# A decoder trunk in Strassen-Winograd products: C11 built on a PSUM copy, another order of loads and branch sums, and two merging additions by accumulating transfers

## The chip, the cores and the metric

The kernel runs on one core of one Trainium2 chip. The metric is device time in microseconds (us), the median of three runs: 780.66 us before the change (779.02 to 780.73). The engines are PE (TensorE, matrix multiply), ACT (ScalarE), DVE (VectorE), POOL (GpSimd) and SP (SyncE, which issues transfers). SP and POOL each have a queue of transfers of their own; the same 16 DMA engines serve both.

## The reference, cut to what matters

```python
# D_MODEL 1024, SEQ 512, DEPTH 1, 16 heads of 64, window 128, D_FF 4096, all float32
h = rmsnorm(x, attn_norm_g)
u_b, u_c, u_x, q, k, v, g_conv, g_attn = split(h @ w_in)
y_conv = (u_b * short_conv(u_c * u_x, conv_w)) @ w_conv_out
attn   = sliding_window_attention(q, k, v, attn_sinks, rel_bias)
y_attn = attn @ w_attn_out
mixed  = sigmoid(g_conv) * y_conv + sigmoid(g_attn) * y_attn
x = x + mixed @ w_o
h2 = rmsnorm(x, mlp_norm_g)
x = x + square(relu(h2 @ w_up)) @ w_down
return rmsnorm(x, final_norm_g)
```

The merge of the two branches, `mixed`, and the five products around it (`g_conv`, `g_attn`, `y_conv`, `y_attn`, `mixed @ w_o`) are the part that the change touches.

## The kernel before, in words

**The first 232 us.** x is normed and transposed; w_in's columns for k, v, q and the convolution go through `transposed_strip`, with the attention of four blocks of 128 queries woven in (`mixer_block`). In the last block `transpose_probs(3, qd)` and `values(3, qd)` for the quads qd = 2 and 3 are left over and are issued among the products that follow. POOL's `mask(n, qd)` zeroes the part of the transposed probabilities outside the window; it is an affine select of the high part, then one of the low part, and `values` waits for both.

**The stages.** From then on the work is 13 stages, each a product of a 512 x 1024 by a 1024 x 1024 matrix: GC and GA (the two gates), CO and AO (the outputs of the two branches), WO (the output projection), then four pairs of w_up and w_down slices. Each stage is one level of Strassen-Winograd: seven products named M1, N2, M6, M5, M7, M3, N4, in this order on PE. The moving operands are B11, B21, T2, T1, T3, B22 and T4, where B11 to B22 are the four blocks of the weights (1 MB each) and T1 to T4 are sums of them. The stationary operands are corners of the activations or sums of them (S1 to S4). For GC and GA, which share their activations, these sums are made once, written to memory, and brought back by SP (`load_sum`, 1 MB for each of M6, M5, M7 and M3) when the attention's tiles under them are free: that of M7 after `values(3, 3)`.

**Two parts of each operand.** A float32 number is split in a high and a low part. ACT makes the high part (`high_part` for weights, L1133; `s_high` for activations, L1210), DVE subtracts it for the low part (`low_part`, L1679; `s_low`, L1734). A product is three kinds: high by high, activation low by weight high, activation high by weight low. Each kind is eight matrix multiplies of 128 x 512, four for each half b of the tokens. The tile `high` has two buffers, so the high part of product n waits until product n-2 has ended.

**The sums of the weights.** T2 = B11 + T3 (`sum_t2`, L1656) and T4 (`sum_t4`, L1673) are DVE additions. T1 and T3 are made by transfers that POOL issues: T3 as one accumulating transfer onto B12 (L612), T1 as a plain transfer (L631) and, when that has landed, an accumulating one onto it (L635). In stage GC the second transfer of T1 stands behind the last `mask` in POOL's program.

**The results.** A stage's four corners are C11 = M1 + N2, C12, C21 (the end of the chain N4) and C22. M1, M6, M7 and N4 accumulate on one pair of PSUM banks, the chain; N2 has a pair of its own, M5 and M3 the third. ACT copies M1 to zc11, M1 + M6 (negated) to zc12 and M5 to zc22 (`copy_out`, L1223), and DVE adds the rest: `sum_c11` (L1824), `sum_c22` (L1830), `sum_c12` (L1835). PE waits for `sum_c22` before it issues N4, since that sum reads the chain.

**The merge.** In GC and GA the corners go through a sigmoid (`gate`). `gate_conv` (L1851) multiplies the corners of CO by the first gate, `gate_attn` (L1858) those of AO by the second, and `merge` (L1865) adds the two on DVE, in the order of corners C11, C22, C12, C21 (numbers 0 to 3). PE transposes each merged corner (`mixed_transposes`, L826): corner 0 behind M5 of AO, corner 1 inside N4 of AO, corners 2 and 3 inside M1 of WO.

**What sets the order.** Every engine's program is written out by hand, and each instruction waits on semaphores. Nothing is reordered at run time: an instruction that waits holds all behind it on its engine. After WO the stages repeat one pattern.

Of the kernel before, what the change touches and what calls it, by code (L numbers as in the profile page):

```python
# [12 lines left out]
P = 128  # L13
# [108 lines left out]

def slot_of(s, i):

    return part_no(s, i) % 3
# [54 lines left out]
def build(nc, x, attn_norm_g, w_in, conv_w, w_conv_out, attn_sinks, rel_bias, w_attn_out, w_o,  # L180
          mlp_norm_g, w_up, w_down, final_norm_g, out):
    ctx = ExitStack()
    with ctx:
# [44 lines left out]
        slot_at = [two_at + 2 * KT * T * i for i in range(3)]  # L228
# [15 lines left out]
        b2_sum, b1_sum = (place(n, [P, 4, 2 * P], offset=two_at + 6 * KT * T + o) for n, o in  # L244
                          (("b2_sum", 0), ("b1_sum", KT * T)))
# [88 lines left out]
        mix_t, mix_ready = sem("mix_t"), sem("mix_ready")  # L334
# [10 lines left out]
        copied, summed, relu_done = sem("copied"), sem("summed"), sem("relu_done")  # L345
# [63 lines left out]
        def sum_of(s, which):  # L409

            return {2: b2_sum, 1: b1_sum}[which] if s < WO else {2: m2_sum, 1: m1_sum}[which]
# [11 lines left out]
        def attn_gate(at_):  # L423

            part, (i, j) = at_ % 2, ((1, 0), (0, 0))[at_ // 2]
            return four_of(gates[:, part, :, :], i, j)
# [28 lines left out]
        def _(sp):  # L455
# [114 lines left out]
        def _(pool):  # L570
# [45 lines left out]
            for n in range(1, TB):  # L616
                if n == 2:
                    add_t3(GC)
                for qd in range(QUADS if n < TB - 1 else QUADS - 1):
                    mask(n, qd)  # L620

            for s in range(STAGES):
# [28 lines left out]
        def _(pe):  # L651
# [219 lines left out]
            def product(s, i, fresh, between={}):  # L871
# [4 lines left out]
                else:  # L876
# [46 lines left out]
            for s in range(STAGES):  # L923
                if is_up(s):
# [17 lines left out]
                    pe.wait_ge(summed, 3 * g + 2)  # L942
                    up_product(s, N4, False)
                    continue
                if s < WO:
                    if s == GA:
                        pe.wait_ge(pv_out, QUADS * TB)
                    elif s == CO:
                        pe.wait_ge(summed, 1)
                    elif s == AO:  # L950
                        pe.wait_ge(summed, 3 * GA + 1)
                    product(s, M1, True)
                    if s == GC:
# [21 lines left out]
                    pe.wait_ge(copied, 3 * s + 3)  # L975
                    product(s, M3, False)
                    pe.wait_ge(summed, 3 * s + 2)
# [4 lines left out]
                pe.wait_ge(summed, 3 * up_no(s - 1) + 1)  # L982
# [12 lines left out]
                pe.wait_ge(summed, 3 * up_no(s - 1) + 3)  # L995
# [13 lines left out]
        def _(act):  # L1009
# [125 lines left out]
            def mixer_block(n, it, before):  # L1135
# [26 lines left out]
                probs_hi(n, 1)  # L1162
                lo_share(n, 1)
# [7 lines left out]
            def gate(s, at_):  # L1171

                i, j = CORNERS[at_]
                if at_ < 3:
                    act.wait_ge(summed, 3 * s + at_ + 1)
# [15 lines left out]
            def s_high(s, i):  # L1191
# [14 lines left out]
                if at_ < 3:  # L1206
                    wait_used(act, GA, {M1: M5, N2: M7, M6: M3}[i])
# [928 lines left out]
```

## Time and profile before

| what | value |
|---|---|
| three runs, median (lowest, highest) | 780.66 us (779.02, 780.73) |
| the profiled execution's own time | 779.52 us |
| its span, first to last instruction | 777.7 us |
| mean granted TensorE clock | 0.991 |
| PE busy | 751.2 us, 97% |
| DVE busy | 650.7 us, 84% |
| ACT busy | 418.4 us, 54% |
| POOL busy | 82.9 us, 11% |
| PE idle before stationary loads of the products, put down to "issue" | 11.9 us |

A row of the timeline gives the start in us, the duration, the engine, the line of the kernel, the operation with output and input, and, in square brackets, how long the engine sat idle before it and what ended that. A matmul row's duration overlaps the next by a part, since matmuls are pipelined: the distance of two starts tells more than the duration. One kind of a product goes by in 1.81 us, a product in 5.44 us, at full clock.

### The profile page before, as it was taken

Reading aid. Unit: us, or ns where it says so; the run is one execution under the profiler, and the core shown is the slowest. Engines: PE = TensorE matmul, PEld = TensorE weight load, DVE = VectorE, ACT = ScalarE, POOL = GpSimd, SP = SyncE. Lnnn points to the kernel's source line nnn. Section 1 sums busy time; section 2 is a strip of 40 time slices with the busy share of each in tenths; the row PEclk is TensorE's granted clock in tenths of the full one; section 3 lists DMA queues with packets and bytes.
Section 4 is the critical chain, followed back from the end, with each engine's and each line's share of the span. In section 5 each row is a group of like instructions: output and inputs, shape, how many; then the busy total and the mean of one; then the engine's idle time right before and its main releaser. Section 6 shows DMA issues by size and latency. Waiting matters only on the chain.

```text
span 777.7 us, 10470 instructions
## 1 busy us (share of the span) xinstructions
PE 751.2 (97%) x4067; PEld 649.5 (84%) x4067; DVE 650.7 (84%) x752; ACT 418.4 (54%) x530; POOL 82.9 (11%) x117
## 2 busy tenths in 40 slices
PE   8999999999999499999997999999999999999996
PEld 7888888888887388887785899988998899889985
DVE  5766788988897365989999899998699969995997
ACT  7424555544534355665564778554555455535456
POOL 3202000111014010101010100101010101010102
PEclk9999999999999799999999999999999999999999
DMA  7737413161238776767592766677767767777702
GB/s 258 231 99 267 149 55 108 55 163 54 81 112 300 183 208 163 217 173 212 187 279 76 176 184 182 169 208 177 204 165 195 184 181 198 188 191 193 207 7 109
DMA packets 69408, 131.22 MB, mean 169 GB/s; under 512 B 2604, under 2 KB 22132, under 8 KB 69364
## 3 DMA queue, kind: packets, MB, share of 16 engines
q1 hardware_dynamic: 50400, 84.18, 32.7%
q0 software_dynamic: 18752, 46.15, 26.9%
q8 instruction: 30, 0.49, 0.2%
q10 hardware_dynamic: 212, 0.28, 0.1%
q14 instruction: 14, 0.11, 0.1%
HBM read 124.29 MB, written 6.32 MB: 168 GB/s over the span
## 4 chain that ended last, share of the span: by engine, by line
PE 83%; DVE 9%; issue 3%; DMA 2%; ACT 1%; POOL 0%; SPq 0%; DVEq 0%; ACTq 0%
PE pair L898 35%; PE pair L863 21%; PE pair L672 7%; PE pair L674 7%; PE pair L673 7%; DVE home_lo L1679 2%; DMA home_raw<-in_w_attn_out 2%; PE pair L719 1%; DVE s_lo_tile L1734 1%; PE pair L694 1%; DVE home_raw L1673 1%; PE pair L693 1%; PE pair L703 1%; DMA xn<-in_x 1%; DVE home_raw L1656 1%
## 5 line engine op out<-in xcount | busy, mean ns | idle before, releaser
L1133 ACT ACTIVATE high<-home_raw 128x2048 fp32r<-128x2048 f32 x91 | 174.3, 1915 | 172.6 <-PE pair L898 114.8
L1679 DVE TENSOR_TENSOR home_lo<-home_raw,high 128x2048 fp32r<-128x2048 f32 x91 | 208.5, 2291 | 47.1 <-ACT high L1133 46.7
L898 PE MATMUL pair<-high,s_hi_tile 128*128 128x512 f32 x440 | 111.9, 396 | 11.9 <-issue 9.8
L898 PE MATMUL pair<-high,s_lo_tile 128*128 128x512 f32 x440 | 111.3, 394 | 2.9 <-DVE s_lo_tile L1734 2.9
L898 PE MATMUL pair<-home_lo,s_hi_tile 128*128 128x512 f32 x440 | 110.3, 392 | 0.5 <-DVE home_lo L1679 0.5
L898 PEld LDWEIGHTS pair<-high,s_hi_tile 128*128 128x128 f32 x440 | 82.8, 190 | 30.4 <-issue 11.9
L672 PE MATMUL pair<-h,wgt 128*128 128x512 f32 x256 | 101.5, 397 | 0.0
L898 PEld LDWEIGHTS pair<-high,s_lo_tile 128*128 128x128 f32 x440 | 83.3, 190 | 21.2 <-DVE s_lo_tile L1734 3.8
L674 PE MATMUL pair<-h,wgt 128*128 128x512 f32 x256 | 99.9, 390 | 0.0
L673 PE MATMUL pair<-h,wgt 128*128 128x512 f32 x256 | 99.8, 390 | 0.0
L898 PEld LDWEIGHTS pair<-home_lo,s_hi_tile 128*128 128x128 f32 x440 | 83.1, 189 | 18.3 <-DVE home_lo L1679 0.9
L863 PE MATMUL pair<-h_hi,home_lo 128*128 128x256 f32 x448 | 58.4, 283 | 0.0
L863 PE MATMUL pair<-h_lo,high 128*128 128x256 f32 x448 | 58.4, 283 | 0.0
L863 PE MATMUL pair<-h_hi,high 128*128 128x256 f32 x448 | 58.3, 283 | 0.0
L674 PEld LDWEIGHTS pair<-h,wgt 128*128 128x128 f32 x256 | 48.1, 188 | 10.5
L863 PEld LDWEIGHTS pair<-h_hi,high 128*128 128x128 f32 x448 | 56.0, 192 | 0.3
L673 PEld LDWEIGHTS pair<-h,wgt 128*128 128x128 f32 x256 | 48.2, 188 | 9.2
L863 PEld LDWEIGHTS pair<-h_hi,home_lo 128*128 128x128 f32 x448 | 55.8, 192 | 0.0
L863 PEld LDWEIGHTS pair<-h_lo,high 128*128 128x128 f32 x448 | 55.8, 192 | 0.0
L672 PEld LDWEIGHTS pair<-h,wgt 128*128 128x128 f32 x256 | 48.1, 188 | 9.1
L1465 DVE TENSOR_TENSOR wgt<-raw,wgt 128x1024 fp32r<-128x1024 f32 x33 | 39.0, 1221 | 8.6 <-ACT wgt L1027 8.4
L1027 ACT ACTIVATE wgt<-raw 128x1024 fp32r<-128x1024 f32 x33 | 33.2, 1056 | 21.2 <-PE pair L674 21.1
(211 smaller groups left out, 1007.9 us busy)
## 6 DMA issues: line engine op xcount, KB each, us to landing
raw<-in_w_in SPq DMA_DIRECT2D x34, 512.0 KB, 4.6
home_raw<-in_w_up SPq DMA_DIRECT2D x16, 1024.0 KB, 5.5
home_raw<-in_w_down SPq DMA_DIRECT2D x16, 1024.0 KB, 5.4
home_raw<-in_w_up POOLq DMA_DIRECT2D x12, 1024.0 KB, 8.1
home_raw<-in_w_down POOLq DMA_DIRECT2D x12, 1024.0 KB, 8.5
home_raw<-in_w_in POOLq DMA_DIRECT2D x7, 1024.0 KB, 8.8
home_raw<-in_w_in SPq DMA_DIRECT2D x7, 1024.0 KB, 5.1
home_raw<-in_w_conv_out SPq DMA_DIRECT2D x4, 1024.0 KB, 5.1
```

The source lines that it names most:

```text
L672: mm(bank[j][:, :], wh, rhs[:, 0, k, :], start=(k == 0), stop=False)
L673: mm(bank[j][:, :], wh, rhs[:, 1, k, :], start=False, stop=False)
L674: last = mm(bank[j][:, :], wl, rhs[:, 0, k, :], start=False, stop=(k == KT - 1))
L693: mm(acc, q, khi[:, kg, keys], start=True, stop=False)
L694: last = mm(acc, q, klo[:, kg, keys], start=False, stop=True)
L703: last = nc.tensor.transpose(bank[B_PT][:, c * P:(c + 1) * P], pr[:, qd % 2, i, P:2 * P], ident[:, :])
L863: last = mm(acc[:, f, :], w[:, k, f * P:(f + 1) * P], a_[:, k, :], start=(fresh and kind == 0 and k == 0 and f % 2 == 0), stop=(kind == 2 ...
L898: last = mm(pair[region(s, i)][:, b, :], a_[:, k, b * P:(b + 1) * P], w[:, k, :], start=(fresh and kind == 0 and k == 0), stop=(kind == 2 ...
L1027: a(wgt[weight_slot(s1)][:, 0, 1024 * e:1024 * e + 1024], raw[raw_slot(c1)][:, :], ACT.Copy).then_inc(hi_ready, 1)
L1133: a(high[n % 2][:, :], home_raw[home_of(s, name)][:, :], ACT.Copy).then_inc(m_hi, 1)
L1465: v.tensor_tensor(w[:, 1, 1024 * e:1024 * e + 1024], raw[raw_slot(2 * s1 + e)][:, :], f32(w[:, 0, 1024 * e:1024 * e + 1024]), ALU.subtract ...
L1679: v.tensor_tensor(home_lo[home][:, :], home_raw[home][:, :], f32(high[n % 2][:, :]), ALU.subtract).then_inc(m_lo, 1)
```

## The change: what it does

1. **C11 on a copy in PSUM** (stages GA, CO, AO). ACT's `seed` copies M1's two halves from the chain to N2's pair, half b when M1's half b has ended. N2 then accumulates on the copy (`fresh` is false), with its kinds in the order high and activation-low of half 0, the same of half 1, then weight-low of both. Its first matmul of half 0 waits for `half_copied`, that of half 1 for `copied`. `copy_out` of M1 and `sum_c11` are gone from these stages; `gate`, `gate_conv` and `gate_attn` read corner 0 in PSUM.
2. **GC's first products.** N2 follows M1 directly; `values(3, 2)` and `transpose_probs(3, 3)` stand behind N2 and `values(3, 3)` behind M6. ACT makes N2's high part earlier, DVE puts `sum_t4` and `low_part(N2)` ahead of `probs_lo(3, 2)`.
3. **Loads.** In GC, POOL issues T1's first transfer ahead of `mask(3, 2)` and its accumulating one ahead of `mask(3, 3)`. SP loads GA's B12 ahead of B11.
4. **Branch sums.** S2 and S1 of CO and AO move to free corners of `gates`, the activation parts get five slots instead of three in these stages (`PART_SLOTS`), and `s_high`, `s_low`, s1 to s4, `gate` and the sums of results stand elsewhere in ACT's and DVE's programs.
5. **Two merges by transfer.** Corners 0 and 1 are added by an accumulating transfer from `gates` to `mixed` (0.5 MB each) that POOL issues: merge(0) behind T1 of AO, merge(1) between the two transfers of T1 of WO. Corners 2 and 3 stay on DVE.

```diff
-    return part_no(s, i) % 3
+    n = part_no(s, i)
+    return PART_SLOTS[n] if n < len(PART_SLOTS) else n % 3
...
+            sp.wait_ge(t_ready, 4 * (TB - 1) + 3)
+            load_sum(HS.index(M5))
+            load_block(GA, 0, 1)
             wait_strip(sp, S_OUT - 1)
             sp.wait_ge(m_lo, 1)
             load_block(GA, 0, 0)
-            sp.wait_ge(t_ready, 4 * (TB - 1) + 3)
-            load_sum(HS.index(M5))
-            load_block(GA, 0, 1)
...
+            def merge(at_):
+
+                pool.wait_ge(weighed, at_ + 1)
+                pool.wait_ge(gated, at_ + 1)
+                pool.dma_start(four_of(mixed, *CORNERS[at_]), attn_gate(at_), accum_op=ALU.add).then_inc(mix_added, 16)
...
                 if s == GC:
-                    mask(TB - 1, QUADS - 1)
+                    mask(TB - 1, 2)
+                if s == WO:
+                    merge(1)
                 pool.wait_ge(t1_base, 16 * (s + 1))
                 pool.dma_start(home_rows(home_of(s, "T1")), weights(s, 0, 1), accum_op=ALU.add).then_inc(t1_in, 16)
+                if s == AO:
+                    merge(0)
+                if s == GC:
+                    mask(TB - 1, 3)
...
-                pe.wait_ge(mix_done, at_ + 1)
+                pe.wait_ge(mix_added, 16 * (at_ + 1)) if at_ < 2 else pe.wait_ge(mix_done, at_ - 1)
...
+                if seeded(s) and i == N2:
+                    order = [(0, 0), (0, 1), (1, 0), (1, 1), (0, 2), (1, 2)]
...
+                    if seeded(s) and i == N2 and kind == 0:
+                        pe.wait_ge(copied, copied_no(s, 1)) if b else pe.wait_ge(half_copied, s)
...
+            def seed(s):
+
+                if s == AO:
+                    act.wait_ge(gated, 4)
                 else:
+                    act.wait_ge(gate_done, 4 * s)
+                for b in range(2):
+                    act.wait_ge(prod, 14 * s + 2 * M1 + b + 1)
+                    a(pair[region(s, N2)][:, b, :], pair[region(s, M1)][:, b, :], ACT.Copy
+                      ).then_inc((half_copied, copied)[b], 1)
```

POOL's program at the head of the stages, before and then after: `pt` is the tile of probabilities that `mask` works on, home_raw_97 and then home_raw_99 the place of T1.

```order
L607 AFFINE_SELECT pt<-pt 128x512 [waits pt_hi]
L607 AFFINE_SELECT pt<-pt 128x512 [waits pt_ready]
L631 DMA home_raw_97<-in_w_in 128x4x512 [waits half_ready1]
L607 AFFINE_SELECT pt<-pt 128x512 [waits pt_hi]
L607 AFFINE_SELECT pt<-pt 128x512 [waits pt_ready]
L635 DMA home_raw_97<-in_w_in 128x4x512 [waits t1_base]
```

```order
L668 DMA home_raw_99<-in_w_in 128x4x512 [waits half_ready1]
L638 AFFINE_SELECT pt<-pt 128x512 [waits pt_hi]
L638 AFFINE_SELECT pt<-pt 128x512 [waits pt_ready]
L674 DMA home_raw_99<-in_w_in 128x4x512 [waits t1_base]
L638 AFFINE_SELECT pt<-pt 128x512 [waits pt_hi]
L638 AFFINE_SELECT pt<-pt 128x512 [waits pt_ready]
```

Each of T1's two transfers stands one `mask` further ahead than it did.

DVE's program in stage GA, from the sum T2 of the next stage (L1656, then L1710) to the sum C22 (the row that writes zc22): L1679 and L1733 are `low_part`, L1734 and L1788 `s_low` of CO. First before, then after.

```order
L1656 TENSOR_TENSOR home_raw_94<-home_raw_92,home_raw_97 128x2048
L1755 SCALAR_TENSOR_TENSOR b_sum<-y 128x1024
L1679 TENSOR_TENSOR home_lo_107<-home_raw_93,high_120 128x2048
L1734 TENSOR_TENSOR s_lo_tile_76<-y,s_hi_tile_73 128x1024
L1830 TENSOR_TENSOR zc_85<-zc_85,pair 128x1024
L1679 TENSOR_TENSOR home_lo_112<-home_raw_98,high_121 128x2048
```

```order
L1710 TENSOR_TENSOR home_raw_96<-home_raw_94,home_raw_99 128x2048
L1733 TENSOR_TENSOR home_lo_109<-home_raw_95,high_122 128x2048
L1788 TENSOR_TENSOR s_lo_tile_82<-y,s_hi_tile_77 128x1024
L1823 TENSOR_TENSOR y<-y,gates 128x4x256
L1788 TENSOR_TENSOR s_lo_tile_78<-gates,s_hi_tile_73 128x1024
L1733 TENSOR_TENSOR home_lo_114<-home_raw_100,high_123 128x2048
L1884 TENSOR_TENSOR zc_89<-zc_89,pair 128x1024
```

Between the T2 sum and the C22 sum stood two small instructions and one `low_part`; now three small ones and two `low_part` stand there, the second that of N4, which came behind the C22 sum.

## Rows read from the trace of the kernel before

**Rows 1.** The page: the chain that ended last, by engine.
```profile
PE 83%; DVE 9%; issue 3%; DMA 2%; ACT 1%; POOL 0%; SPq 0%; DVEq 0%; ACTq 0%
```
**Rows 2.** Timeline of PE, stages GC to WO; idle time in brackets.
```profile
232.63 2.10 PE L898 MATMUL pair<-high,h 128*128 128x512 f32 x8
...
263.81 3.75 PE L898 MATMUL pair<-high,s_hi_tile 128*128 128x512 f32 x8 [9.76 <-issue]
...
287.81 3.79 PE L898 MATMUL pair<-high,h 128*128 128x512 f32 x16
...
298.69 1.98 PE L898 MATMUL pair<-high,g_hi 128*128 128x512 f32 x8
...
325.90 1.98 PE L898 MATMUL pair<-high,s_hi_tile 128*128 128x512 f32 x8
...
359.48 2.11 PE L898 MATMUL pair<-high,s_hi_tile 128*128 128x512 f32 x8 [0.77 <-DVE zc L1830]
...
365.05 1.98 PE L898 MATMUL pair<-high,s_hi_tile 128*128 128x512 f32 x8
...
421.12 3.09 PE L898 MATMUL pair<-high,s_lo_tile 128*128 128x512 f32 x8 [2.46 <-DVE s_lo_tile L1734]
...
438.27 1.98 PE L898 MATMUL pair<-high,s_hi_tile 128*128 128x512 f32 x8
```
**Rows 3.** Timeline of ACT, stages GC and GA.
```profile
239.93 0.60 ACT L1112 ACTIVATE pt<-pair 128x512 fp32r<-128x512 f32 x1
...
261.80 1.91 ACT L1133 ACTIVATE high<-home_raw 128x2048 fp32r<-128x2048 f32 x1 [12.56 <-DMA home_raw<-in_w_in]
...
298.95 1.92 ACT L1133 ACTIVATE high<-home_raw 128x2048 fp32r<-128x2048 f32 x1 [2.61 <-PE pair L898]
```
**Rows 4.** Timeline of POOL, stage GC.
```profile
237.93 0.78 POOL L631 DMA_DIRECT2D home_raw<-in_w_in  x1
240.61 0.88 POOL L607 TENSOR_SCALAR_AFFINE_SELECT pt<-pt 128x512 fp32r<-128x512 f32 x1 [1.90 <-ACT pt L1112]
245.19 2.62 POOL L607 TENSOR_SCALAR_AFFINE_SELECT pt<-pt 128x512 fp32r<-128x512 f32 x1 [3.70 <-DVE pt L1613]
247.76 1.30 POOL L635 DMA_DIRECT2D home_raw<-in_w_in  x1
```
**Rows 5.** Line L635 in 230 to 270 us: issue to landing, one transfer.
```profile
DMA to landing us min/median/max: 14.0/14.0/14.0
```
**Rows 6.** Line L612: issue to landing at 304.1 and at 382.9 us.
```profile
DMA to landing us min/median/max: 8.1/8.1/8.1
DMA to landing us min/median/max: 16.8/16.8/16.8
```
**Rows 7.** Line L635 at 283.2 and at 358 to 361 us: issue to landing.
```profile
DMA to landing us min/median/max: 10.2/10.2/10.2
DMA to landing us min/median/max: 11.6/11.6/11.6
```
**Rows 8.** Stretches: us, busy of each engine, PEclk, DMA share, GB/s.
```profile
258.00:262.00 4.00, 0.00 (x0) 0.00 (x0) 0.00 (x0) 0.20 (x1) 0.00 (x0) 0.52 1.09 288
...
397.00:401.00 4.00, 4.00 (x19) 3.30 (x19) 3.97 (x4) 0.98 (x1) 0.00 (x0) 1.00 0.99 352
...
421.00:425.00 4.00, 3.88 (x11) 3.10 (x12) 4.00 (x5) 2.32 (x3) 0.00 (x0) 0.62 0.00 0
```
**Rows 9.** Timeline of DVE, end of the attention and stage GA.
```profile
234.67 0.84 DVE L1622 TENSOR_TENSOR qa<-pair,pv_low 64x256 f32<-64x256 f32 x2
...
312.35 2.29 DVE L1656 TENSOR_TENSOR home_raw<-home_raw,home_raw 128x2048 f32<-128x2048 f32 x1 [2.87 <-DMA home_raw<-in_w_conv_out]
314.56 1.22 DVE L1755 SCALAR_TENSOR_TENSOR b_sum<-y 128x1024 f32<-128x1024 f32 x1
315.70 2.29 DVE L1679 TENSOR_TENSOR home_lo<-home_raw,high 128x2048 fp32r<-128x2048 f32 x1
...
319.04 1.22 DVE L1830 TENSOR_TENSOR zc<-zc,pair 128x1024 f32<-128x1024 f32 x1
```

More of the change, by code:

```diff
@@ L120, in drained_before, with part_before, seeded, summed_no @@
     return 0 if s == WO else 8 + 6 * ((s - WO) // 2 - 1)
+PART_SLOTS = (3, 4, 0, 1, 2, 3, 4) + (0, 1, 2, 4, 0, 1, 2) + (4, 0, 1, 2, 0, 1, 2)
 def slot_of(s, i):
-    return part_no(s, i) % 3
+    n = part_no(s, i)
+    return PART_SLOTS[n] if n < len(PART_SLOTS) else n % 3
+def part_before(s, i):
+    n, slots = part_no(s, i), [slot_of(p, k) for p in PARTED for k in range(7)]
+    before = [m for m in range(n) if slots[m] == slots[n]]
+    if not before:
+        return GA, {3: M6, 4: M5, 0: M5, 1: M7, 2: M3}[slots[n]]
+    return PARTED[before[-1] // 7], before[-1] % 7
+def seeded(s):
+    return GA <= s <= AO
+def summed_no(s, k):
+    if s > AO:
+        return 9 + 3 * (up_no(s) - 4) + k
+    return 3 * s - max(s - 1, 0) + k - (1 if seeded(s) else 0)
+def copied_no(s, k):
+    return 3 * up_no(s) + k
 def home_of(s, name):
@@ L409, in sum_of @@
         def sum_of(s, which):
-            return {2: b2_sum, 1: b1_sum}[which] if s < WO else {2: m2_sum, 1: m1_sum}[which]
+            if s < WO:
+                return four_of(gates[:, 2 - which, :, :], 1, 0 if s == CO else 1)
+            return {2: m2_sum, 1: m1_sum}[which]
         def part_source(s, i):
@@ L1173, in gate @@
                 i, j = CORNERS[at_]
-                if at_ < 3:
-                    act.wait_ge(summed, 3 * s + at_ + 1)
+                if at_ == 0 and s == GA:
+                    wait_used(act, s, N2)
+                    src = four(region(s, N2))
+                elif at_ < 3:
+                    act.wait_ge(summed, summed_no(s, at_ + 1))
                     src = (zc11, zc22, zc12)[at_]
@@ L1288, in _ @@
             s_high(AO, M3)
+            s_high(AO, N4)
             high_part(AO, M3)
@@ L1877, in relu @@
                                        op1=ALU.mult).then_inc(relu_done, 1)
+            sum_t4(GC)
+            low_part(GC, N2)
             probs_lo(3, 2)
             normalise(3, 3)
-            sum_t4(GC)
-            low_part(GC, N2)
+            low_part(GC, M6)
+            probs_lo(3, 3)
             attention_out(3, 2)
-            probs_lo(3, 3)
-            low_part(GC, M6)
-            attention_out(3, 3)
             sum_c11(GC)
             low_part(GC, M5)
+            attention_out(3, 3)
             low_part(GC, M7)
@@ L1894, in _ @@
             low_part(GA, M1)
+            s3(CO)
+            sum_c12(GC)
             sum_t4(GA)
-            sum_c12(GC)
             low_part(GA, N2)
-            s3(CO)
+            s2(CO)
+            s1(CO)
             low_part(GA, M6)
-            sum_c11(GA)
+            s3(AO)
             low_part(GA, M5)
             low_part(GA, M7)
+            s_low(CO, M1)
             sum_t2(CO)
-            s2(CO)
             low_part(GA, M3)
-            s_low(CO, M1)
+            s_low(CO, N2)
+            s4(CO)
+            s_low(CO, M6)
+            low_part(GA, N4)
             sum_c22(GA)
-            low_part(GA, N4)
-            s_low(CO, N2)
-            s1(CO)
+            s_low(CO, M5)
             low_part(CO, M1)
+            s_low(CO, M7)
             sum_c12(GA)
@@ L1934, in _ @@
             gate_conv(1)
-            s_low(AO, M1)
+            s_low(AO, M6)
+            low_part(AO, M1)
             sum_c12(CO)
-            low_part(AO, M1)
             gate_conv(2)
-            s_low(AO, N2)
             gate_conv(3)
@@ L1942, in _ @@
             low_part(AO, N2)
-            s_low(AO, M6)
-            s1(AO)
             low_part(AO, M6)
-            s4(AO)
             s_low(AO, M5)
-            sum_c11(AO)
+            gate_attn(0)
             low_part(AO, M5)
-            gate_attn(0)
-            merge(0)
             s_low(AO, M7)
```

138 lines of the change are left out of this document (64 added, 74 removed).

## The prediction, made before the changed kernel ran

> **What bounds the kernel now.** I read the chain of waits first: PE holds 83% of it, DVE 9%, "issue" 3% [rows 1]. So only idle time of PE, slow stretches of its clock, and what DVE makes it wait for can be won; work taken from ACT, DVE or POOL counts only where PE waits for it. The timeline of PE then shows where it stands still in the stages that the change touches [rows 2]. The reader is to see one large hole, 9.76 us ahead of M5 of stage GC at 263.81, and small ones around the merge, the largest 2.46 us at 421.12. Between 263.81 and 415 PE loses hardly a us: seven products of stage GA take 325.90 - 287.81 = 38.09 us, so 5.44 us each and 1.81 us a kind. Third, the engines behind the holes. The hole in GC says "issue", but ACT's high part of M5 starts at 261.80, after 12.56 us of waiting for a transfer of w_in, which is T1 [rows 3]. T1's accumulating transfer was issued at 247.76, behind `mask(3, 3)`, whose last select began at 245.19 [rows 4], and took 14.0 us to land [rows 5]. Last, the clock: 0.52 in the second half of that hole, and 0.62 at 421 to 425, after holes of the merge [rows 8]. M5's first kind took 3.75 us [rows 2].
>
> All sums are against the profiled execution, 779.52 us for a span of 777.7; the median of the three runs, 780.66, lies 1.1 us above it.
>
> **Stage GC: minus 12.0 us.** With the new order POOL issues T1's first transfer when the last strip has ended, at 231.4 (M1 of GC starts at 232.63, behind 1.3 us of values and transposes [rows 2]) instead of 237.93 [rows 4]. The accumulating one then waits for `mask(3, 2)`, which waits for `probs_lo(3, 2)` on DVE, now behind `sum_t4` and `low_part(N2)`: two big DVE instructions, 2.2 us each back to back (312.35 to 314.56; a small one takes 1.13, 314.56 to 315.70 [rows 9]), from the end of the row at 234.67, 235.5, give 240.0, the low half 0.6, the select 0.9, so 241.4 for the issue instead of 247.76. Landing: 8.1 us for 1 MB accumulated alone [rows 6], 10.2 and 11.6 with another load beside it [rows 7], 14.0 in the old place, where four sums, a block and T3 went with it [rows 5]. Now block B22 goes beside it and the sums only later: I take 10.6, landing at 252.0, plus ACT's 1.9 [rows 3]: M5 can start at 254.0. PE gets there as follows: M1 from 232.6, N2, quad 2's values and transposes (1.3), M6, quad 3's values (0.9): 232.6 + 3 x 5.44 + 2.2 + 0.1 = 251.3. So a wait of 2.7 is left, then four products: GA's M1 starts at 254.0 + 21.8 = 275.8 instead of 287.81 [rows 2]. What is late next is M7's sum, loaded only after `values(3, 3)`, at 251.4; it has until 259.4, 8 us for 1 MB beside T3's transfer, against 8.1 to 11.6 for such pairs above: 0 to 3 us, taken 0. Bounds: 14.7 us gained with 8.1 to the landing (no wait then), 8.6 with 14.0, and 2 less if the hole slows the clock.
>
> In a sentence apart: the select at 245.19 took 2.62 us while DVE ran, that at 240.61 took 0.88 [rows 4]. The Trainium skill (SBUF — State Buffer, "Who interferes with whom") says that a DVE instruction with two SBUF inputs and a GpSimd instruction that reads SBUF exclude each other; by it the select would take 2.6 where DVE goes on with `low_part`, and GC would gain 1.7 less; I keep 0.9 since small instructions of `normalise` follow there.
>
> **The seeds: plus 0.15 us, and plus 0.95 in CO.** Before, M1 was copied out beside N2. Now N2 waits for the copy of half 0. That half ends one group of four matmuls (0.9 us) before M1 does; ACT starts on a product's end 0.26 us after the next one's first matmul (298.95 [rows 3] against 298.69 [rows 2]); the copy of 128 x 512 out of PSUM is 0.60 at 239.93, into SBUF [rows 3]; into PSUM no row shows it, from 0.5 to 1.0 (twice the elements). 0.26 + 0.6 + 0.1 against 0.9 leaves 0.1; with 1.0 it is 0.5 a stage. Half 1 has 1.8 us more. The seed also stands behind ACT's queue: in GA after a high part and two gates, done 4.1 us into M1, in time. In CO it is late, see below.
>
> **GA: plus 3.3 us.** Here an order speaks against the change. PE issues N4 only when `sum_c22` has read the chain. DVE's T2 sum for the next stage began at 312.35, held by a transfer 2.87 us [rows 9], 24.5 us into the stage; the transfer follows N2, so it stays there. Before, between it and the end of `sum_c22` stood 2.2 + 1.13 + 2.2 + 1.13 + 1.13 = 7.8: the sum began at 319.04 and was out at 320.2, just as M3 ended, at 325.90 - 5.44 = 320.46 [rows 2, 9]. Now DVE first does `s_low(M1)` (to 24.85), T2's sum, `low_part(M3)`, three small ones, `low_part(N4)`, then `sum_c22`: 24.85 + 3 x 2.2 + 4 x 1.13 = 36.0 us into the stage. M3 ends at 6 x 5.44 + 0.15 = 32.8. N4 waits 3.2; the stage becomes 38.1 + 0.15 + 3.2, 3.4 longer with rounding. Its follower: gate 1 on ACT waits for the same sum, gate 2 and CO's high part of N2 stand behind it, so CO's seed starts 0.9 us after half 0 of M1 is there: the 0.95. At CO's own N4 `sum_c22` is about as late as before, 0.77 us at 359.48 [rows 2]; 0.9 is taken. CO: 38.1 + 0.95 + 0.9 = 39.95 against 365.05 - 325.90 = 39.15: plus 0.8. DVE's bounds: plus 2.5 to 4.5 for GA, plus 0 to 1.5 for CO.
>
> **AO and WO: plus 0.2 us.** Before, from AO's M1 to WO's M7 438.27 - 365.05 = 73.22 us passed, the hole of 2.46 with its smaller neighbours among them, and 4 us at 0.62 of the clock [rows 8], 1.5 us lost. DVE loses the additions for C11 (three of 1.13) and two merges (1.2 each). Corner 0 is weighed 13.3 us into the stage and needed at 21.9; corner 1 is weighed at 30.9 and needed at 35.5, after N4's first kind. An accumulating transfer of 0.5 MB from SBUF to SBUF is in no row. Below it lies a DVE merge, a small instruction, 1.2 us [rows 9]; above it 1 MB in this very stretch, 16.8 us [rows 6], where DMA is busy at 0.99 to 401 [rows 8] and T1, residual and blocks queue up. I take 8.1, the lone 1 MB: half the bytes, in traffic. Corner 0 lands at 21.4, in time. Corner 1 lands at 39.0: PE waits 3.5 inside N4. Behind it: ACT's mixed copy and high part, DVE's low part, gate 2, merge 2, low part, gate 3, merge 3, in a row; WO's N2 starts some 13.6 us after the transposes of corner 1, its kind 1 at 15.9 (`s_low` is now ahead of s3 and s2), M6 at 21.1 (held by S2 and its high part), M7 at 33.5. With the transposes done at 39.9 that is 73.4. Each us by which corner 1 is earlier, down to 3.5, comes back whole.
>
> In a sentence apart: the Trainium skill (DMA: Bandwidth & Descriptors, "Anatomy of one DMA — SWDGE (gpsimd) path") gives 2.0 us plus the bytes over 436 GB/s, 3.2 us for 0.5 MB; by it corner 1 would land at 34.1, in time, and the stage pair would win 3.3; no row here shows a transfer that small on POOL's queue.
>
> **Clock: plus 2.3 us.** The slow stretch after WO's holes I leave (its 1.5 is in 73.22, so nothing new); for the new holes of 2.7, 3.2 and 3.5 us, of which the first 4 us of the old hole passed at full clock and the rest not [rows 2, 8], I add 2.3, between 0 and 5.
>
> **Sum.** -12.0 + 3.4 + 0.8 + 0.2 + 2.3 = -5.3. 779.5 - 5.3 = 774.2 on the profile's scale, 775.3 on that of the median. From WO's M7 on nothing is changed, and DVE is as far ahead there as before.
>
> **Rivals.**
> 1. *The transfers are quick.* T1 lands in 8.1, corner 1 before 35.5: GC gains 14.7, AO and WO 3.3, little clock: -14.7 + 3.4 + 0.8 - 3.3 + 1 = -12.8, so 768. For it: T1 meets fewer loads than before. Against it: 16.8 and 11.6 in the rows. Half of it (one of the two) gives 771.
> 2. *T1's wait stays.* The transfer takes 14.0 as before, or `mask(3, 2)` is 2 us late, and the clock falls: GC gains 6 instead of 12: 781. For it: DMA is at 1.09 in the old hole; against it: what filled it comes later now.
> 3. *The merging transfers are slow* (the other side). Both take 16.8 as POOL's did at 382.9 [rows 6]. Corner 0 lands at 30.1, PE stands 8.2 us ahead of M7; corner 1 is weighed 8.2 later and lands at 55.9 against 43.7 needed, 12.2 more, 8.7 above the 3.5 in the sum: 775.3 + 16.9 = 792. It decides from about 11 us a transfer on, where the two waits eat the 5.3. For it: the same queue and stretch; against it: half the bytes, no memory outside to read, and corner 0 issued before most of the loads.
> 4. *The copy in PSUM is not free*: 1.0 us a half and late seeds, 3 x 0.5 more: 777; inside the forecast.
>
> **Chances.** Forecast with rival 4: 0.55, own range 771.5 to 779. Rival 1: 0.25. Rival 2: 0.12. Rival 3: 0.08. A measurement of this kernel can tell 0.3%, 2.3 us, from no change. Faster (below 778.3): 0.92 of the first, all of the second, 0.2 of the third: 0.78. Same: 0.12. Slower: 0.10. The range 768 to 782 leaves out rival 3, half the tail of rival 1 and a bit of rival 2.
>
> **What would show it right or wrong.** Right: T1's accumulating transfer issued near 241.4, a hole of at most 4 us ahead of GC's M5, GA's M1 near 276; a wait of PE for `sum_c22` of 2.5 to 4 us at GA's N4, the sharpest claim here; a first-kind wait for the seed below 0.5 in GA and near 1 in CO; landings of the merges near 8 us and a hole of 2 to 5 us inside AO's N4, none ahead of AO's M7. Wrong: T1 landing after 256, no wait at GA's N4, a merge that lands after 11 us, or new waits behind WO's M7.

## The result, and the profile after

The changed kernel takes 783.91 us (median of 9 runs, 782.24 to 785.89), the kernel before 779.47 in the runs beside it (9 runs, 776.48 to 780.73). The ratio is 1.0058, with a 95% interval of 1.0043 to 1.0073: slower by 4.4 us. Forecast were 775.3 us and a range up to 782. The profiled execution took 783.21 us for a span of 781.5, 3.8 us more than the span of before.

On the page, the chain that ended last now holds 5% of DMA, where it held 2% [rows 1]. Its second line names tiles that no transfer of the kernel before joined, `mixed<-gates`:

```profile
PE 86%; DVE 7%; DMA 5%; issue 2%; ACT 0%; POOL 0%; SPq 0%; DVEq 0%; POOLq 0%; ACTq 0%
PE pair L945 35%; PE pair L906 21%; PE pair L715 8%; PE pair L717 7%; PE pair L716 7%; DMA mixed<-gates 2%; DVE home_lo L1733 2%; DMA home_raw<-in_w_conv_out 2%; PE pair L762 2%; DMA s_lo_tile<-h_sums 1%; DVE s_lo_tile L1788 1%; PE pair L737 1%; PE pair L736 1%; PE pair L746 1%; PE pair L774 1%
```

The timeline of PE, read beside [rows 2], shows where the time went. Here are the holes and the starts of the stages (GA's M1 at 278.04, CO's M1 at 321.89, AO's M1 at 361.67, WO's M7 at 442.03):

```profile
254.41 2.14 PE L945 MATMUL pair<-high,s_hi_tile 128*128 128x512 f32 x8 [2.84 <-ACT high L1175]
...
261.60 2.08 PE L945 MATMUL pair<-high,s_hi_tile 128*128 128x512 f32 x8 [1.42 <-DMA s_lo_tile<-h_sums]
...
278.04 3.79 PE L945 MATMUL pair<-high,h 128*128 128x512 f32 x16
...
314.77 5.48 PE L945 MATMUL pair<-high,h 128*128 128x512 f32 x16 [3.81 <-DVE zc L1884]
...
321.89 1.98 PE L945 MATMUL pair<-high,s_hi_tile 128*128 128x512 f32 x8
...
356.09 2.11 PE L945 MATMUL pair<-high,s_hi_tile 128*128 128x512 f32 x8 [1.28 <-DVE zc L1884]
...
361.67 1.98 PE L945 MATMUL pair<-high,s_hi_tile 128*128 128x512 f32 x8
...
385.47 1.07 PE L869 MATMUL pair<-ident,mixed 128*128 128x128 f32 x8 [1.74 <-DMA mixed<-gates]
...
406.12 1.97 PE L869 MATMUL pair<-ident,mixed 128*128 128x128 f32 x8 [6.16 <-DMA mixed<-gates]
...
442.03 1.98 PE L945 MATMUL pair<-high,s_hi_tile 128*128 128x512 f32 x8
```

Differences of these starts give the stages, all in us of profiled executions:

| | before | predicted difference | measured difference | after |
|---|---|---|---|---|
| GA's M1 starts | 287.81 | -12.0 | -9.77 | 278.04 |
| GA (M1 to CO's M1) | 38.09 | +3.4 | +5.76 | 43.85 |
| CO | 39.15 | +0.8 | +0.63 | 39.78 |
| AO's M1 to WO's M7 | 73.22 | +0.2 | +7.14 | 80.36 |
| slow clock | | +2.3 | inside the rows above | |
| sum | | -5.3 | +3.76 | |

The sum is the whole difference of the spans, so behind WO's M7 nothing changed. GC gave most of what it was to give; AO and WO took it away.

Four groups show how. POOL in GC, to be read against [rows 4], and the landing of T1's accumulating transfer, 10.7 where it was 14.0 [rows 5]:

```profile
231.87 0.79 POOL L668 DMA_DIRECT2D home_raw<-in_w_in  x1 [0.84 <-PE pair L717]
236.66 1.69 POOL L638 TENSOR_SCALAR_AFFINE_SELECT pt<-pt 128x512 fp32r<-128x512 f32 x1 [4.01 <-ACT pt L1154]
241.16 0.64 POOL L638 TENSOR_SCALAR_AFFINE_SELECT pt<-pt 128x512 fp32r<-128x512 f32 x1 [2.81 <-DVE pt L1667]
241.75 1.29 POOL L674 DMA_DIRECT2D home_raw<-in_w_in  x1
...
DMA to landing us min/median/max: 10.7/10.7/10.7
```

VectorE (DVE) in GA, against [rows 9]: between the T2 sum and `low_part(N4)` (311.30) stand four instructions, and the sum of c22 (L1884) comes behind them, at 313.50.

```profile
303.28 2.29 DVE L1710 TENSOR_TENSOR home_raw<-home_raw,home_raw 128x2048 f32<-128x2048 f32 x1 [0.45 <-DMA home_raw<-in_w_conv_out]
305.49 2.29 DVE L1733 TENSOR_TENSOR home_lo<-home_raw,high 128x2048 fp32r<-128x2048 f32 x1
307.69 1.22 DVE L1788 TENSOR_TENSOR s_lo_tile<-y,s_hi_tile 128x1024 fp32r<-128x1024 f32 x1
309.02 1.23 DVE L1823 TENSOR_TENSOR y<-y,gates 128x1024 f32<-128x1024 f32 x1
310.16 1.22 DVE L1788 TENSOR_TENSOR s_lo_tile<-gates,s_hi_tile 128x1024 fp32r<-128x1024 f32 x1
311.30 2.28 DVE L1733 TENSOR_TENSOR home_lo<-home_raw,high 128x2048 fp32r<-128x2048 f32 x1
313.50 1.22 DVE L1884 TENSOR_TENSOR zc<-zc,pair 128x1024 f32<-128x1024 f32 x1
```

DVE in AO. WO's T2 sum (L1710) waits 6.31 us for T3's transfer of w_o, issued at 378.55 and landed in 15.7 us. The sum of c22 (L1884) and the weighing of corner 1 (L1913) stand behind it:

```profile
385.77 2.29 DVE L1733 TENSOR_TENSOR home_lo<-home_raw,high 128x2048 fp32r<-128x2048 f32 x1
394.37 2.29 DVE L1710 TENSOR_TENSOR home_raw<-home_raw,home_raw 128x2048 f32<-128x2048 f32 x1 [6.31 <-DMA home_raw<-in_w_o]
396.58 1.21 DVE L1884 TENSOR_TENSOR zc<-zc,pair 128x1024 f32<-128x1024 f32 x1
397.83 1.23 DVE L1913 TENSOR_TENSOR gates<-gates,zc 128x1024 f32<-128x1024 f32 x1
```

The two merging transfers (line L657, issued at 375.40 and 399.42), issue to landing:

```profile
DMA to landing us min/median/max: 9.9/9.9/9.9
...
DMA to landing us min/median/max: 6.6/6.6/6.6
```

And the clock around the two large holes, in the columns of [rows 8]:

```profile
312.00:316.00 4.00, 1.23 (x3) 1.04 (x4) 3.85 (x3) 1.25 (x2) 0.87 (x1) 0.84 0.95 268
316.00:320.00 4.00, 4.00 (x14) 3.21 (x14) 2.37 (x2) 2.55 (x2) 0.00 (x0) 0.73 1.05 189
401.00:405.00 4.00, 0.00 (x0) 0.00 (x0) 1.38 (x2) 0.00 (x0) 1.02 (x1) 0.81 1.18 243
405.00:409.00 4.00, 2.88 (x11) 2.69 (x12) 0.00 (x0) 0.88 (x1) 0.00 (x0) 0.50 1.11 201
```

GA's N4, two kinds of matmuls in one row, took 5.48 us instead of 3.79: the hole of 3.81 costs 1.7 more. In AO, PE had nothing to do from 399.96 to 406.12; the clock fell inside this hole (0.81 over 401 to 405) and stood at the lower of its two levels, 1.2 GHz, from 405 to 409 (0.50).

### The profile page after: what moved, and what is told of

The parts are those of the page before. It is cut to its first block, busy times and chain, and to the rows that moved or that the text cites. A ratio compares the mean times of both kernels' runs of the same rounds, so it can differ in the third digit from the quotient of the medians.

```text
span 781.5 us, 10469 instructions
## 1 busy us (share of the span) xinstructions
PE 752.3 (96%) x4067; PEld 650.5 (83%) x4067; DVE 645.6 (83%) x747; ACT 418.6 (54%) x533; POOL 84.2 (11%) x119
## 4 chain that ended last, share of the span: by engine, by line
PE 86%; DVE 7%; DMA 5%; issue 2%; ACT 0%; POOL 0%; SPq 0%; DVEq 0%; POOLq 0%; ACTq 0%
PE pair L945 35%; PE pair L906 21%; PE pair L715 8%; PE pair L717 7%; PE pair L716 7%; DMA mixed<-gates 2%; DVE home_lo L1733 2%; DMA home_raw<-in_w_conv_out 2%; PE pair L762 2%; DMA s_lo_tile<-h_sums 1%; DVE s_lo_tile L1788 1%; PE pair L737 1%; PE pair L736 1%; PE pair L746 1%; PE pair L774 1%
## 5 line engine op out<-in xcount | busy, mean ns | idle before, releaser
L1733 DVE TENSOR_TENSOR home_lo<-home_raw,high 128x2048 fp32r<-128x2048 f32 x91 | 208.3, 2290 | 46.5 <-ACT high L1175 46.1
```

The lines of the kernel that those rows point to most:

```text
L1733: v.tensor_tensor(home_lo[home][:, :], home_raw[home][:, :], f32(high[n % 2][:, :]), ALU.subtract).then_inc(m_lo, 1)
```

## The experiments

All times are medians; the ratio is to runs of the kernel before on the same chip (779.59 us for e1 to e4, 780.12 for e5 to e8, 780.62 for e9 to e12; each of these three groups ran on a chip of its own, so between groups the ratios compare better than the times). Stage lengths come from one profiled execution each.

**e1: GC's part alone.** The edit is the change's order on SP, POOL, PE, ACT and DVE inside GC, on the kernel before.

> Only the part of the change in GC (loads of T1 and the order of GC's sums, copies and products); GA, CO, AO and WO stay as before. Theory (the step of GC holds, the loss lies in the later stages): GA's first product starts about 9.8 us earlier than in the kernel before, as in the changed kernel, nothing after it gives it back: 769.5 to 771 us, ratio to before 0.987 to 0.989. Rival (the clock or a later wait gives part of GC's gain back whatever the later stages do): 773 to 777 us, and a stage after GA's first product is longer than before by 3 us or more.

Measured: 769.7 us, ratio 0.9869 [0.9842, 0.9897], inside the theory's figures. GA's M1 starts at 277.72; GA is 38.40, CO 39.48, AO and WO 73.10 us long, as before within 0.4. So the whole gain of GC reaches the end when the later stages leave it alone. The change held a kernel 10 us faster than the one before and 14 faster than itself.

**e12: POOL's order alone.** Of e1, this keeps only:

```diff
-                for qd in range(QUADS if n < TB - 1 else QUADS - 1):
+                for qd in range(QUADS if n < TB - 1 else 2):
...
-                    mask(TB - 1, QUADS - 1)
+                    mask(TB - 1, 2)
                 pool.wait_ge(t1_base, 16 * (s + 1))
                 pool.dma_start(home_rows(home_of(s, "T1")), weights(s, 0, 1), accum_op=ALU.add).then_inc(t1_in, 16)
+                if s == GC:
+                    mask(TB - 1, 3)
```

> The kernel before with POOL's order alone changed: T1's accumulating transfer stands behind mask(3, 2) instead of mask(3, 3); the loads of SyncE and the orders of the other engines stay. In the changed kernel it landed in 10.7 us, in the kernel before in 14.0. If the traffic beside it makes the difference (four sums, a block and T3 go with it here, as before), it still takes 13 to 14 us from its issue near 241.5 to 245: M5 starts at 257 to 260, 3 to 5 us less than before, 774.5 to 776.5 us. If it is the place in POOL's queue alone, it lands in 10 to 11 us and the time is 771 to 773 us.

Measured: 769.95 us, ratio 0.9859 [0.984, 0.9879], as good as e1. Its accumulating transfer was issued at 243.22 and landed in 9.3 us with SP's order of loads unchanged:

```profile
243.22 1.31 POOL L635 DMA_DIRECT2D home_raw<-in_w_in  x1 [5.04 <-DMA home_raw<-in_w_in]
...
DMA to landing us min/median/max: 9.3/9.3/9.3
```

SP's new order of loads is thus not needed for the short landing. T3's transfer and the four sums are issued 3.2 to 5.9 us behind it here (246.44 to 249.07), 0.8 to 2.7 behind it in the kernel before (248.54 to 250.50); that the transfer is further on when it meets them is the likely reason, argued from these times only. The total lies below the figures of both theories, nearer to those of the place in POOL's queue. In this profile (771.1 us, the slowest of its four runs) PE waits 2.52 us for M5 and 2.22 for M7's sum. How much the orders of the other engines in GC are worth beyond POOL's can't be told from two medians 0.25 us apart, taken on two chips.

**e4: merges 0 and 1 back on DVE.** On the changed kernel:

```diff
-                pe.wait_ge(mix_added, 16 * (at_ + 1)) if at_ < 2 else pe.wait_ge(mix_done, at_ - 1)
+                pe.wait_ge(mix_done, at_ + 1)
...
             gate_attn(0)
+            merge(0)
...
             gate_attn(1)
+            merge(1)
```

> The changed kernel with the merging additions 0 and 1 done by VectorE again, as before, behind the weighing of their corner; the rest of the orders stays. Theory A (the late weighing is the larger part of the loss of AO and WO, a merging transfer costs its own 6.6 to 9.9 us of latency on top): the addition takes some 2 us in place of the transfer's 6.6, so the hole before the transposes of corner 1 shrinks from 6.16 to 1 to 3 us, but the weighing still comes after the T2 sum (6 us of waiting for DMA in that place): 779 to 781 us. Rival B (the transfers alone are the loss): AO and WO come back to what they were before, 776 to 777.5 us. Rival E (VectorE is late behind the T2 sum and has four microseconds more to do): no gain, 783 to 786 us.

Measured: 777.28 us, ratio 0.9972 [0.9958, 0.9987], 6.6 us less than the changed kernel. AO and WO are 73.80 instead of 80.36, and 73.22 before the change. The T2 sum still waits 6.30 us, and N4 now shows it as a wait for c22. The hole ahead of the transposes of corner 1 is 0.41:

```profile
397.78 2.11 PE L935 MATMUL pair<-high,s_hi_tile 128*128 128x512 f32 x8 [2.32 <-DVE zc L1874]
400.30 1.09 PE L859 MATMUL pair<-ident,mixed 128*128 128x128 f32 x8 [0.41 <-DVE mixed L1910]
```

Total and stages are those of rival B, and the hole of 0.41 is smaller than theory A had it. But the wait of the T2 sum that A names is there; what it costs, e7 shows.

**e5: the two merging transfers on top of e1**, with VectorE's order as before, less the two merges.

> The kernel with GC's part alone (769.7 us) plus the two merging transfers of the change, and nothing else: VectorE's order stays that of the kernel before, less merge(0) and merge(1). Theory B (a merging transfer costs its own 6.6 to 10 us from issue to landing, against 1.2 us on VectorE, and PE waits for what is more than its slack): corner 0 is weighed 20 us into AO and its transposes stand at 22.9, so they wait 4 to 8 us; corner 1 waits 1 to 5 us; 7 to 11 us more than 769.7, so 776.5 to 781 us. Rival A (the transfers are cheap, it was the order of VectorE around them): 769 to 773 us.

Measured: 779.15 us, ratio 0.9989 [0.9977, 1.0001]: 9.45 us more than e1, inside theory B's figures. In the profiles AO and WO are 8.2 longer (81.30 against 73.10). Here the T2 sum of WO stands where it stood before, behind the weighing. The transfers landed in 9.1 and 6.0 us:

```profile
387.00 1.94 PE L838 MATMUL pair<-ident,mixed 128*128 128x128 f32 x8 [7.70 <-DMA mixed<-gates]
388.59 3.59 PE L910 MATMUL pair<-high,s_hi_tile 128*128 128x512 f32 x8
...
404.88 1.09 PE L838 MATMUL pair<-ident,mixed 128*128 128x128 f32 x8 [1.78 <-DMA mixed<-gates]
```

The first hole brings a slow clock (1.94 for transposes that took 1.04, 3.59 for a kind of 2.09). DVE, which was to gain by the transfers, stood still for 11.81 us behind them, waiting for PE.

**e2: WO's T2 sum behind the weighing**, on the changed kernel:

```diff
             low_part(AO, M3)
-            sum_t2(WO)
             sum_c22(AO)
             gate_attn(1)
             low_part(AO, N4)
+            sum_t2(WO)
```

> The changed kernel with one move: on VectorE WO's sum_t2 stands behind the weighing of corner 1 and low_part(AO, N4) instead of ahead of AO's sum of c22. Theory A (corner 1 is weighed late because the T2 sum ahead of it waits for T3's transfer of w_o): the weighing comes about 6.3 us earlier, the second merging transfer is issued near 394 on the changed kernel's clock and the transposes of corner 1 wait 0 to 2 us instead of 6.16; with the slow clock behind the hole gone, 776.5 to 779 us (5 to 7 us off the changed kernel). Rival B (the merging transfers themselves are the loss: they take what they take whenever they are issued, or slow down when they meet T3's transfer): the merging transfer takes 10 us or more, the hole stays above 3 us, 781 to 784 us.

Measured: 782.73 us, ratio 1.0046 [1.0029, 1.0063], 1.2 us less than the changed kernel. That was a miss, and the total is rival B's: the profile shows 3.6 us less (AO and WO 76.78), but it is that of the fastest of the eight runs. The transposes of corner 1 wait 1.97 us, as theory A said, with the transfer landing in 6.2. But the weighing came 2.3 us earlier into the stage, not 6.3: the sum of c22 now waits for PE, which is late itself, since corner 0's transfer took 10.5 us, made a hole of 2.34 and a slow clock behind it:

```profile
386.75 1.06 PE L869 MATMUL pair<-ident,mixed 128*128 128x128 f32 x8 [2.34 <-DMA mixed<-gates]
387.56 3.26 PE L945 MATMUL pair<-high,s_hi_tile 128*128 128x512 f32 x8
...
404.09 1.09 PE L869 MATMUL pair<-ident,mixed 128*128 128x128 f32 x8 [1.97 <-DMA mixed<-gates]
```

N4 starts 37.8 us into AO here, in the changed kernel 36.2: what the T2 sum no longer holds up, corner 0's transfer does.

**e3: GA's sum of c22 directly behind `low_part(M3)`**, on the changed kernel (s4 and `s_low(M6)` of CO move behind `low_part(N4)`).

> The changed kernel with one move: in GA the sum of c22 stands directly behind low_part(M3) on VectorE. Theory D (GA's loss is N4's wait for that sum and the slow clock that follows the hole): N4's hole of 3.81 us goes, and with it 1 to 2 us of slow clock; GA is 38 to 39 us instead of 43.85, total 778 to 780 us. Rival (the seeded copy or the first loads make GA longer, or N4 finds the next wait, its low part, in place of this one): GA stays at 41 us or more, total 781 to 784 us.

Measured: 781.53 us, ratio 1.0033 [1.0017, 1.0048], 2.4 us less. N4 has no wait and GA is 38.20 long, 5.65 less, as theory D said; the total misses D's 778 to 780. CO is 42.29, 2.5 more, since PE now waits for the seed, and AO and WO are 81.75, 1.4 more (corner 1's transfer took 8.1):

```profile
324.35 1.19 PE L945 MATMUL pair<-high,s_hi_tile 128*128 128x512 f32 x4 [2.32 <-ACT pair L1264]
```

ACT shows why. Gate 2 waits for the sum of c12, and a high part, gate 3 and the seed stand behind it:

```profile
319.91 1.06 ACT L1230 ACTIVATE gates<-zc 128x1024 f32<-128x1024 f32 x1 [5.80 <-DVE zc L1889]
320.88 1.90 ACT L1175 ACTIVATE high<-home_raw 128x2048 fp32r<-128x2048 f32 x1
322.69 1.00 ACT L1230 ACTIVATE gates<-pair 128x1024 f32<-128x1024 f32 x1
323.72 1.07 ACT L1264 ACTIVATE pair<-pair 128x512 f32<-128x512 f32 x2
```

In the changed kernel GA's hole had hidden this wait, as CO's M1 came later.

**e7: the edits of e2, e3 and e4 together.**

> The changed kernel with its three suspects removed together: merges 0 and 1 on VectorE, WO's sum_t2 behind the weighing of corner 1, GA's sum of c22 directly behind low_part(M3). The seeded copy stays. If the three are the whole loss apart from the wait for CO's seed that GA's move opened (2.32 us), AO and WO are 73 to 74 us and the total is 772 to 774 us. If a fourth cause exists (seeds in all stages, the loads), 775 us or more. Without any cost of the seed it would be 769.5 to 771 us.

Measured: 771.08 us, ratio 0.9889 [0.9866, 0.9913], a little below the figures. AO and WO are 70.54, 2.7 shorter than before, where the prediction's working without transfers gave 3.3. With the merges on DVE, the T2 sum's place is therefore worth 73.80 - 70.54 = 3.3 us. CO is 44.23, 4.5 longer than in the changed kernel: the wait that e3 opened ahead of N2 is here too, with slow kinds behind it.

```profile
323.70 1.63 PE L935 MATMUL pair<-high,s_hi_tile 128*128 128x512 f32 x4 [2.53 <-ACT pair L1254]
```

**e8: the same without the copy in PSUM**, M1 copied out and added as before.

> As the kernel with the three suspects removed, and the copy in PSUM undone too: M1 is copied to SBUF and added by VectorE, N2 starts fresh, as in the kernel before. Theory C (the seed costs what PE waits for it: 0.1 us a stage where ScalarE is free, 2.3 us at CO's N2 where its queue is behind gate 2): 1.5 to 2.5 us less than with the seed, 769.5 to 772 us. Rival (the three more additions of 1.13 us on VectorE make a wait elsewhere, so the seed pays for itself): equal or slower, 772 to 775 us.

Measured: 771.93 us, ratio 0.9899 [0.9878, 0.9921], 0.85 more than with the seed, which the intervals don't tell from nothing; theory C said 1.5 to 2.5 less, and the rival was nearer. The wait at CO's N2 stays, 2.51 us: without a seed N2 waits for gate 3 (`ACT gates L1221`), which stands in the same queue. The hole was never the seed's.

**e9: e7 with GA's sum of c12 directly behind `low_part(GA, N4)`.**

> The kernel with the three suspects removed (771.08 us) and GA's sum of c12 directly behind low_part(GA, N4) on VectorE. Theory F (the wait of 2.53 us ahead of CO's N2 is that sum's place: ScalarE's gate 2 waits 6 us for it, and the high part, gate 3 and the seed stand behind gate 2): the wait goes, with 1.2 us of slow clock behind it: 767 to 768.5 us. Rival (ScalarE is late for another reason, or DVE's later parts are now late for CO's M1): 770 us or more.

Measured: 767.51 us (5 runs, 767.37 to 769.05), ratio 0.9844 [0.9829, 0.9859]; the best kernel here, 12 us faster than before and 16 faster than the change. CO is 39.79. N2 follows M1 at once, the seeds run beside PE:

```profile
321.38 1.18 PE L935 MATMUL pair<-high,s_hi_tile 128*128 128x512 f32 x4
```

**e11: e9 without the copy in PSUM.**

> As the kernel with c12 moved, without the copy in PSUM (M1 copied to SBUF, added by VectorE, N2 fresh). With no wait left in front of CO's N2 this gives the seed's own worth: 0.1 us of PE a stage lost by the seed against 1.13 us of VectorE a stage won. If PE never waits for VectorE in these places: equal within 0.5 us, 767 to 768.5 us. If VectorE's time counts, 1 to 3 us slower without the seed.

Measured: 767.66 us, ratio 0.9838 [0.9822, 0.9854]: no difference. What the seed takes from DVE is nothing that PE waited for.

**e10: e9 with merges 0 and 1 by transfer again.**

> The same orders as the last kernel, but merges 0 and 1 by accumulating transfers as in the change. Every wait around them is gone, so this is the price of the two transfers alone, issued as early as their corners are weighed. Theory B (6 to 10 us each against a slack of some 8 us for corner 0 and 4 for corner 1; 6.6 us were lost to them in the changed kernel): 5 to 7 us more than with VectorE's merges, 773 to 775 us. Rival (with the corners weighed early the transfers are hidden): within 1.5 us of it, 768 to 769.5 us.

Measured: 776.58 us, ratio 0.9955 [0.9939, 0.9971], 9.1 us more than e9, worse than expected. The profiled run is its fastest (773.97 us) and shows 6.35 of it: AO and WO 76.83 against 70.48. No transfer stands ahead of the weighing of either corner, and both holes are there, with landings of 10.1 and 6.7:

```profile
379.92 1.85 PE L869 MATMUL pair<-ident,mixed 128*128 128x128 f32 x8 [1.88 <-DMA mixed<-gates]
381.42 3.02 PE L945 MATMUL pair<-high,s_hi_tile 128*128 128x512 f32 x8
...
397.79 1.09 PE L869 MATMUL pair<-ident,mixed 128*128 128x128 f32 x8 [2.44 <-DMA mixed<-gates]
```

**e6: e1 with WO's `s_low(N2)` ahead of s3 and s2**, one more piece of the change.

> GC's part alone (769.7 us) plus one more piece of the change: WO's s_low(N2) stands ahead of the branch sums s3 and s2 on VectorE. The wait of 2.48 us ahead of WO's N2 kind 1 goes and with it about 1.5 us of slow clock (its first kind took 3.59 us); the branch sum for M6 is one short instruction later, so a wait of about 1.4 us opens there, as in the changed kernel. 767.5 to 769 us. Rival (what is won is lost again ahead of M6, or the clock dips there instead): 769.3 to 770.5 us.

Measured: 768.76 us, ratio 0.9859 [0.9839, 0.988], 0.9 below e1. In the profile the 2.48 us wait and the slow kind are gone, and 1.37 stand ahead of M6, as expected; AO to WO's M7 is 1.5 shorter. The difference of the medians is too small to be told from nothing. Nor is the 1.5 the order's for certain: e12 has the order of before in these stages and the same wait, and took 71.62 as e6 did (71.61), since no slow kind followed there:

```profile
414.36 2.14 PE L900 MATMUL pair<-high,s_lo_tile 128*128 128x512 f32 x8 [2.48 <-DVE s_lo_tile L1736]
```

## Why the prediction was wrong

**The step that failed** is "AO and WO: plus 0.2 us"; the two stages took 7.14 more. It failed in two places.

First, "corner 1 is weighed at 30.9". That takes the corner to be ready when PE has it, and in e7 it is: the weighing is done 31.0 us into the stage. In the changed kernel it is done at 37.4. The edit also puts WO's T2 sum ahead of it on DVE, and that sum waits for T3's transfer of w_o. The landing of that transfer, 16.8 us, was in [rows 6]; the prediction used it for a rival about the merging transfers and not for the sum that waits for it. PE came to corner 1 at 38.3, so its transfer had 0.9 us of slack and not 4.6; it took 6.6 and not 8.1, landed at 44.4 and not 39.0, and PE waited 6.16 and not 3.5. The price of this place is 3.3 us without the merging transfers (e4 against e7); with them 1.2 by the medians (e2) and 3.6 in the profile.

Second, "Corner 0 lands at 21.4, in time". The price of a merging transfer, 8.1, was right as a mean: in five profiled kernels corner 0's took 9.1 to 10.5 us and corner 1's 6.0 to 8.1. But corner 0 had 8 us. It was issued 13.7 us into the stage and landed 23.6, not 21.4, so PE stood 1.74 us. In the changed kernel this alone cost nothing: N4 starts 36.18 us into the stage there and 36.23 in e4, where corner 0 is in time, since in both the sum of c22 behind the T2 sum sets it. It counts as soon as the T2 sum is out of the way, which is why e2 won so little. The prediction charged the transfers 3.5 us, for corner 1 alone; they cost 6.6 by the medians and in the profiles (e4), all of it behind the start of N4, and 9.1 to 9.45 by the medians where the T2 sum was out of the way (e10, e5; 6.35 and 8.2 in the profiles). In the profiles: -2.7 for the orders, +3.3 for the T2 sum, +6.6 for the transfers make the +7.14 of the table. Of the 2.7, 1.6 is the slow clock behind WO's hole of 2.46 [rows 2], which e7 lacks and which e12, with the orders of before, lacks too (71.62 instead of 73.22).

**GC** held, with an error of 2.2 us. T1's accumulating transfer was issued at 241.75 (241.4 foretold), landed in 10.7 (10.6), M5 started at 254.41 (254.0). M7's sum, taken at 0, was 1.42 late, inside the bound of 3. Of the reason given for the shorter landing, that the sums go later, one half fell: SP's new order isn't needed (e12). That the sums start further behind the transfer holds in e12 too and stays the likely cause, not a shown one.

**GA** was the sharpest claim, and the mechanism was right: N4 waits for the sum of c22, 3.81 us instead of 3.2. With 1.7 of slow clock and the seed it is +5.76. e3 shows it alone: the edit gives back 5.65 in GA. What the prediction did not see is that the same queue holds the next wait, for c12 through gate 2, which comes out when GA is quick.

**CO** (+0.63 for +0.8) was right in size and half wrong in cause: N4's wait was 1.28; the seed was not late, as CO's M1 was itself.

**The seeds** were priced rightly. A half took 0.58 us from PSUM to PSUM, and N2 is about 0.1 us late:

```profile
282.83 0.58 ACT L1264 ACTIVATE pair<-pair 128x512 f32<-128x512 f32 x1 [0.76 <-PE pair L945]
283.68 0.58 ACT L1264 ACTIVATE pair<-pair 128x512 f32<-128x512 f32 x1 [0.26 <-PE pair L945]
```

Rival 4 (the copy not free) is refuted by e11. A reading that nothing in the sum rests on was too low: between 263.81 and 415 PE lost not "hardly a us" but 2.4 us in four waits (0.77, 0.48, 0.48 and 0.69), and 2.2 more in M5's first two kinds, which were still slow.

The select that the Trainium skill's rule (SBUF — State Buffer, "Who interferes with whom") would have made 2.6 us took 0.64. In that stretch DVE has only short instructions, so this select is no test of the rule. Two others are, which began while DVE was at a big one with two inputs, the first in the kernel before, the second in the changed one:

```profile
245.03 2.28 DVE L1679 TENSOR_TENSOR home_lo<-home_raw,high 128x2048 fp32r<-128x2048 f32 x1
...
235.56 2.29 DVE L1727 TENSOR_TENSOR home_raw<-home_raw,home_raw 128x2048 f32<-128x2048 f32 x1
```

The selects at 245.19 [rows 4] and 236.66 took 2.62 and 1.69 us, and each ended 0.50 after that instruction's end. This is as the rule has it.

**The clock**: 1.7 in GA, and 2.1 in AO behind the hole of 6.16 (1.97 for transposes of 1.04, 3.30 for a kind of 2.09), less 1.6 behind the hole of 2.46 that is gone ([rows 2], 3.09 and the 2.65 after it): 2.2 in sum, against 2.3 foretold. That this is near is luck. The 2.3 was for new holes alone, and the new holes cost 3.8: nothing behind the one ahead of GC's M5, 1.7 in GA, and 2.1 behind a hole in AO of 6.16 where 3.5 was foretold; the 1.6 that went was counted as staying. Of rival 3 the sign came true but not the price: it needed transfers of 11 us or more, and 6.6 and 9.9 were enough, as a second wait stood in front of one of them.

The formula quoted from the Trainium skill (DMA: Bandwidth & Descriptors, "Anatomy of one DMA — SWDGE (gpsimd) path") gave 3.2 us for 0.5 MB. Here no merging transfer took less than 6.0. All ran beside loads: over 401 to 405 us the DMA share is 1.18 while 243 GB/s move. But load isn't the whole reason. In the kernel before, the accumulating transfer of 304.1 [rows 6] runs with no other from 306.5 to 311.5, and in that time 194 GB/s move at a DMA share of 1.09, where over 397 to 401, with plain loads among the traffic, 352 move at 0.99 [rows 8]. By these rows 0.5 MB less takes some 2.7 us off the lone 8.1, so some 5.4 for a lone merging transfer: an estimate, which no run tests.

What stays open: why corner 0's transfer takes some 3 us more than corner 1's (in e3 2 us). Beside the first, two loads of w_o are issued on POOL's queue, two on SP's and the residual between 375 and 386 us; beside the second one on each. No run took these away. Nor is it shown why e10's median lies 2.6 us above its profiled run. Its other three runs had a mean granted clock of 0.992, the profiled one 0.994, which makes 1.5 us of it by an estimate (0.002 of 774); a spread of the landings would do the rest.

## What to carry to other kernels

When an order is rewritten, walk each queue once more with the waits of what moved. An instruction that itself waits for a transfer (here the T2 sum) makes everything put behind it wait as well, and the landing time of that transfer is a number to look up, not the instruction's own 2.3 us. Handing a short addition to an accumulating transfer would here have paid only with some 10 us to spare: it trades 1.2 us of an engine with slack for 6 to 10 us of latency on the path. Take a compound change apart before judging it: here one change of order on POOL's queue held 10 us of gain, and the rest lost 14.

## What the runs showed that was not expected

- An accumulating transfer of 1 MB issued at 243.2 instead of 247.8, with SP's loads as they were, landed in 9.3 instead of 14.0 us: 4.5 us in the issue bought 9.2 in the landing.
- A short hole can have a price beyond itself, and its length doesn't say whether. Ahead of transposes, behind holes of 1.88 (e10) and 2.34 us (e2) the next kind took 3.02 and 3.26 us; behind the 1.74 of the changed kernel it took 2.09, as behind none, and so it did behind the 2.44 of e10. Ahead of GC's M5, holes of 2.84 (changed kernel) and 3.05 (e7) were followed by first kinds of 2.14 and 2.11, holes of 2.39 (e1) and 2.50 (e9) by 3.37 and 3.48. A difference of 1 to 2 us between two profiles can be this alone.
- The copy from PSUM to PSUM on ACT (128 x 512, 0.58 us) is no dearer than the one into SBUF (0.60, [rows 3]).
